# Moving half of an embedding gate from one token block's expert rows to the next block's

## The chip, the core and the metric

The kernel runs on one core of a Trainium2 chip. The metric is device time in microseconds (us) of one launch; less is better. TensorE (PE) does matmuls, VectorE (DVE) and ScalarE (ACT) elementwise work, GpSimd (POOL) issues the gathers and SyncE (SP) the weight loads. All of them run their own instruction streams and meet at semaphores.

## The reference

Two layers over 256 tokens of width 1024, all float32. Each layer has a token mixer (attention, pooling and a gated DeltaNet, merged by gates) and then a channel mixer, which is where the change lies:

```python
h = layer_norm(alpha*h + mixer(h))
q = (h @ w_q)                                    # 8 heads, two halves of 128
# top 16 + top 16 of 128 keys each, top 16 of their sums -> idx, softmax -> wts
act = gelu(einsum('thkd,td->thk', u_tab[idx], h))
ffn = einsum('thk,thkd->td', act * wts, v_tab[idx])
ple = sigmoid(h @ ple_gate) * (p @ ple_proj)     # the embedding gate
h = layer_norm(alpha*h + ffn + ple)
```

Each token reads 8 heads x 16 experts, and each expert is one row of `u` and one of `v`, 2 x 1024 numbers that lie side by side in memory.

## The kernel before, in words

The 256 tokens are two blocks of 128. Within a layer the token mixer comes first. Then come the expert rows: 128 of block 0 (head r = 0..7, rank i = 0..15, written (r, i) below), then 128 of block 1. One "row" is one gather of 128 x 2048 floats, 1 MB: for each of the 128 tokens the expert of that head and rank.

A row passes through four engines. POOL issues the gather into one of 8 slots (L670 in block 0, L688 in block 1) when the slot's earlier row has been weighed (`row_used`). DVE takes the dot product of the `u` half with `h` (L1692, L1722). ACT makes gelu(dot), times the weight, and a 128x128 diagonal matrix of it (L1289 to L1293; L1313 to L1319). PE multiplies the diagonal with the `v` half, two 512-column matmuls that add into `acc`, a PSUM tile of 128x1024 (L894, L913); each matmul shows as two in the trace, so a row is x4. Beside the dot products DVE chooses the experts of a head two ahead, in small pieces, one behind each row; ACT's exponential for it swaps the activation table twice a head, behind row 12.

Block 0's rows are written out row by row, in an order that `steps()` lists; `beside` puts other work behind chosen rows: queries and scores of later heads, the embedding projection (`pp`, L1158), and the embedding gate. The gate is 8 quarters: for each half c of the 1024 columns four quarters j of the contraction (`("pgw", c, j)`, 8 matmul records each, L789), for both blocks of tokens at once. Step `("pg", c, b)` is then ACT's sigmoid out of PSUM (L1449) and DVE's merge: `base = base*gate` (L1927) and `base = alpha*h + base` (L1928). `ACT_STEPS` and `DVE_STEPS` take it one and two rows later than it stands in the list. The quarters of c = 0 are behind rows (5,7), (5,12), (5,15), (6,4) and those of c = 1 behind (6,6), (6,9), (6,12), (7,4). Their weights come by SP, 0.5 MB a quarter (L612): seven of the eight before the rows, the last when the first quarter has been multiplied.

Between the blocks `acc` changes owner: DVE waits for block 0's last matmul, adds `acc` to `base[:, 0]` (L1675), and only then may PE start block 1, with an identity matmul that puts `base[:, 1]` into `acc` (L906).

Block 1's rows are loops: a `Fori` over heads on POOL (8 turns) and PE (7), ACT and DVE (6); the heads at the end are written out again. DVE normalises block 0 beside head 6 and makes the next layer's first columns beside head 7. Then block 1 is normalised and the next layer starts.

## Time and profile before

| | us |
|---|---|
| median of 3 runs | 1884.93 |
| lowest, highest | 1883.52, 1886.23 |
| span of the profiled execution | 1882.7 |
| PE busy | 1708.0 (91%) |
| DVE busy | 1367.7 (73%) |
| ACT busy | 905.3 (48%) |
| POOL busy | 682.3 (36%) |

The profiled execution's own time is known by its span, 1882.7 us from the first to the last instruction; the timed runs lie 0.8 to 3.5 us above that. The page counts an engine as busy while one of its instructions runs. "DMA share" is how much of the time the core's 16 DMA engines had a packet under way, and GB/s is what they moved. The page's slices are 47 us each: slices 6 to 19 are layer 1's expert rows (about 294 to 938 us), slices 26 to 39 layer 2's (about 1227 to 1872 us). In a timeline the brackets say how long the engine had been idle and what ended that; `<-DMA` means that the gather's landing did, so such a start is also the landing's time.

### The profile page before, as it was taken

Reading aid. Unit: us, or ns where it says so; the run is one execution under the profiler, and the core shown is the slowest. Engines: PE = TensorE matmul, PEld = TensorE weight load, DVE = VectorE, ACT = ScalarE, POOL = GpSimd, SP = SyncE. Lnnn points to the kernel's source line nnn. Section 1 sums busy time; section 2 is a strip of 40 time slices with the busy share of each in tenths; the row PEclk is TensorE's granted clock in tenths of the full one; section 3 lists DMA queues with packets and bytes.
Section 4 is the critical chain, followed back from the end, with each engine's and each line's share of the span. In section 5 each row is a group of like instructions: output and inputs, shape, how many; then the busy total and the mean of one; then the engine's idle time right before and its main releaser. Section 6 shows DMA issues by size and latency. Waiting matters only on the chain.

```text
span 1882.7 us, 26286 instructions
## 1 busy us (share of the span) xinstructions
PE 1708.0 (91%) x7264; PEld 980.8 (52%) x7264; DVE 1367.7 (73%) x3499; ACT 905.3 (48%) x2247; POOL 682.3 (36%) x585
## 2 busy tenths in 40 slices
PE   8999999999999878878799999999999998887876
PEld 7987887544444222223389778865443432322222
DVE  5887768877777777776468876687777787777754
ACT  5656543444444444445355665335445454444443
POOL 0110003444344455555311100044444455555553
PEclk9999999999999999999999999999999999999999
DMA  6543769999999999999955347799999999999997
GB/s 247 182 126 134 259 231 402 416 427 426 427 426 413 427 427 428 427 428 427 411 180 169 125 163 243 265 413 410 427 426 427 426 408 420 427 427 428 427 427 306
DMA packets 106728, 660.59 MB, mean 351 GB/s; under 512 B 11888, under 2 KB 12288, under 8 KB 40064
## 3 DMA queue, kind: packets, MB, share of 16 engines
q0 software_dynamic: 75376, 546.57, 69.3%
q1 hardware_dynamic: 31248, 112.74, 17.8%
q8 instruction: 52, 0.85, 0.2%
q14 instruction: 52, 0.43, 0.1%
HBM read 658.20 MB, written 1.06 MB: 350 GB/s over the span
## 4 chain that ended last, share of the span: by engine, by line
PE 46%; DMA 23%; issue 16%; DVE 8%; ACT 5%; POOL 1%; DVEq 1%; ACTq 0%; POOLq 0%; SPq 0%
PE acc L894 12%; DMA arena<-experts_dram,idxu 11%; DMA cst<-experts_dram,stage 8%; PE psum L726 5%; PE psum L727 5%; PE psum L728 5%; PE acc L913 4%; DMA arena<-experts_dram,stage 4%; PE psum L757 3%; PE psum L789 2%; DVE arena L1692 2%; PE acc L726 1%; PE acc L727 1%; PE acc L728 1%; PE psum L816 1%
## 5 line engine op out<-in xcount | busy, mean ns | idle before, releaser
L913 PE MATMUL acc<-arena 128*128 128x512 f32 x896 | 443.9, 624 | 115.3 <-ACT arena L1319 112.5
L894 PE MATMUL acc<-arena 128*128 128x512 f32 x896 | 412.0, 601 | 24.7 <-ACT arena L1293 24.5
L688 POOL DMA_INDIRECT arena<-experts_dram,stage x224 | 299.4, 1337 | 228.5 <-PE acc L913 166.7
L1722 DVE CUSTOM_DVE_ANT_0 arena<-arena,h 128x1024 f32<-128x1024 f32 x224 | 274.7, 1226 | 141.5 <-issue 61.9
L913 PEld LDWEIGHTS acc<-arena 128*128 128x128 f32 x896 | 158.9, 194 | 397.4 <-issue 397.3
L1692 DVE CUSTOM_DVE_ANT_0 arena<-arena,h 128x1024 f32<-128x1024 f32 x224 | 274.7, 1226 | 119.6 <-DMA arena<-experts_dram,idxu 115.8
L670 POOL DMA_INDIRECT arena<-experts_dram,idxu x224 | 244.9, 1093 | 304.7 <-PE acc L894 269.8
L894 PEld LDWEIGHTS acc<-arena 128*128 128x128 f32 x896 | 163.2, 189 | 252.0 <-issue 153.3
L1571 DVE TENSOR_TENSOR raw_r<-raw,w_hi_r 128x1024 fp32r<-128x1024 f32 x150 | 177.6, 1220 | 64.1 <-ACT w_hi_r L1199 63.4
L1313 ACT ACTIVATE gel<-dots 128x1 f32<-128x1 f32 x256 | 51.9, 203 | 294.6 <-DVE dots L1722 293.5
L1199 ACT ACTIVATE w_hi_r<-raw 128x1024 fp32r<-128x1024 f32 x152 | 153.9, 1053 | 49.9 <-DMA raw<-weights_dram 47.6
L1289 ACT ACTIVATE gel<-dots 128x1 f32<-128x1 f32 x256 | 51.3, 200 | 233.2 <-DVE dots L1692 232.0
L1319 ACT ACTIVATE arena<-cst,gw 128x128 f32<-128x128 f32 x256 | 102.8, 401 | 41.7 <-ACT gw L1316 17.7
L1293 ACT ACTIVATE arena<-cst,gw 128x128 f32<-128x128 f32 x256 | 102.8, 402 | 8.4
L726 PE MATMUL psum<-w_hi_r,hidden_r 128*128 128x512 f32 x256 | 102.0, 398 | 4.3 <-DVE raw_r L1571 3.4
L727 PE MATMUL psum<-raw_r,hidden_r 128*128 128x512 f32 x256 | 100.3, 392 | 0.0
L728 PE MATMUL psum<-w_hi_r,hidden_r 128*128 128x512 f32 x256 | 100.3, 392 | 0.0
L726 PE MATMUL psum<-hidden_r,w_hi_r 128*128 128x256 f32 x320 | 91.4, 286 | 0.0
L727 PE MATMUL psum<-hidden_r,w_hi_r 128*128 128x256 f32 x320 | 90.5, 283 | 0.0
L728 PE MATMUL psum<-hidden_r,raw_r 128*128 128x256 f32 x320 | 90.5, 283 | 0.0
L1316 ACT ACTIVATE gw<-gel,wst 128x1 f32<-128x1 f32 x256 | 75.4, 294 | 24.6 <-ACT gel L1313 1.7
L661 POOL DMA_DIRECT2D lnr<-lnrows_dram x2 | 1.1, 538 | 221.0 <-DVE h L1564 221.0
(296 smaller groups left out, 2710.9 us busy)
## 6 DMA issues: line engine op xcount, KB each, us to landing
raw<-weights_dram SPq DMA_DIRECT2D x168, 512.0 KB, 3.7
arena<-weights_dram SPq DMA_DIRECT2D x20, 512.0 KB, 4.6
w_hi<-weights_dram SPq DMA_DIRECT2D x12, 512.0 KB, 5.0
lnr<-lnrows_dram POOLq DMA_DIRECT2D x4, 1024.0 KB
arena<-experts_dram,idxu POOLq DMA_INDIRECT x224
arena<-experts_dram,stage POOLq DMA_INDIRECT x224
lnr<-cum_dram POOLq DMA_DIRECT2D x2, 1024.0 KB, 9.1
cst<-weights_dram SPq DMA_DIRECT2D x4, 512.0 KB, 5.5
```

The costliest lines, as they stand in the source:

```text
L670: nc.gpsimd.indirect_dma_start(slots[n % RING][:, :], None, experts[:, :], bass.IndirectOffsetOnAxis(idxu[:, n:n + 1], 0)).then_inc(slot_i ...
L688: nc.gpsimd.indirect_dma_start(slots[i % RING][:, :], None, experts[:, :], bass.IndirectOffsetOnAxis(stage[:, i:i + 1], 0)).then_inc(slot_ ...
L726: mm(dst, left[0], right[0], start=start, stop=False)
L727: mm(dst, left[0], right[1], start=False, stop=False)
L728: return mm(dst, left[1], right[0], start=False, stop=stop)
L894: last = mm(acc[:, c * 512:(c + 1) * 512], diag[:, i % 4, :], slots[n % RING][:, D + c * 512:D + (c + 1) * 512], start=n == 0, stop=n == R ...
L913: last = mm(acc[:, c * 512:(c + 1) * 512], diag[:, i % 4, :], slots[i % RING][:, D + c * 512:D + (c + 1) * 512], start=False, stop=ends)
L1199: AC(w_hi[:, n % HIS, :], raw[:, raw_slot(L, piece), :], ACT.Copy).then_inc(w_hi_ready, 1)
L1293: AC(diag[:, i % 4, :], ident, ACT.Copy, scale=gw[:, i:i + 1]).then_inc(diag_ready, 1)
L1571: TT(w_lo[:, s, :], raw[:, s, :], w_hi[:, n % HIS, :].bitcast(F32), ALU.subtract).then_inc(w_lo_ready, 1)
L1692: nc.vector.tensor_tensor_reduce(slot[:, 0:D], slot[:, 0:D], h[:, 0, :], 1.0, 0.0, ALU.mult, ALU.add, dots[:, i:i + 1]).then_inc(dot_ready, 1)
L1722: nc.vector.tensor_tensor_reduce(slots[i % RING][:, 0:D], slots[i % RING][:, 0:D], h[:, b, :], 1.0, 0.0, ALU.mult, ALU.add, dots[:, i:i + ...
```

## The change

- The four quarters of c = 0 go behind (5,7), (5,13), (6,5), (6,11), and their sigmoid and merge stand at (7,0) in the list.
- The four quarters of c = 1 leave block 0. PE makes them in block 1 behind rows (0,4), (0,10), (1,0), (1,6) (`GATE_AT`), six rows apart; ACT's sigmoids go behind row (1,11) and DVE's merge behind row (1,13).
- For that the first `OPENING = 2` heads of block 1 are written out on PE, ACT and DVE, and the loops of these engines do two turns fewer. POOL's loop stays as it is.
- Block 0's upper 512 columns have no gate yet when `acc` must be freed. DVE saves `alpha*h + acc` of these columns in `first_sums`, a free place in `hidden`, where it did `base + acc` before; the merge later adds it to `base*gate`.
- PE puts only the lower half of `base[:, 1]` into `acc` at block 1's start, and the upper half at the first row of its last head, by another wait on `base_ready`, which now counts 4 a layer.

The diff, cut to its core (`gate_quarter` is the body that stood under `kind == "pgw"`, `gate_out` and `gate_in` replace the branches for `pg`; `OPENED` keeps ACT's and DVE's main loops from doing `("pg", 1, b)` again):

```diff
     beside |= {(hd - 3, 6): [("sc", 0, hd), ("sc", 1, hd)] for hd in range(4, EH)}
     beside |= {(4, 12): [("pp", 0, 0), ("pp", 1, 0)], (5, 3): [("pp", 0, 1), ("pp", 1, 1)]}
-    beside |= {at: [("pgw", 0, j)] for j, at in enumerate(((5, 7), (5, 12), (5, 15), (6, 4)))}
-    beside |= {at: [("pgw", 1, j)] for j, at in enumerate(((6, 6), (6, 9), (6, 12), (7, 4)))}
-    beside |= {(6 + c, 5): [("pg", c, 0), ("pg", c, 1)] for c in range(2)}
+    beside |= {at: [("pgw", 0, j)] for j, at in enumerate(((5, 7), (5, 13), (6, 5), (6, 11)))}
+    beside |= {(7, 0): [("pg", 0, 0), ("pg", 0, 1)]}
     for r in range(EH):
         for i in range(TOPK):
             s += [("row", r, i)] + beside.get((r, i), [])
-    s += [("ln2", 0), ("experts", 1), ("ln2", 1)]
+    s += [("pg", 1, 0), ("pg", 1, 1), ("ln2", 0), ("experts", 1), ("ln2", 1)]
     return s
+OPENING = 2
+GATE_AT = ((0, 4), (0, 10), (1, 0), (1, 6))
+GATE_OUT, GATE_IN = 11, 13
 
 
...
         diag = at(17760, 512).rearrange("p (i n) -> p i n", i=4)
         emb_gate = at(18272, 2048).rearrange("p (b d) -> p b d", b=2)
+        first_sums = hidden[:, KT * T:KT * T + 512]
         tiu = sb("tiu", 32, U32)[:, :].rearrange("p (s k) -> p s k", s=2)
         posu = sb("posu", TOPK, U32)
...
                 read(L, g, j, ends[1])
 
+            def gate_quarter(L, c, j):
+                blocks = []
+                for b in range(2):
+                    bk, use = place(L, ("pg", c, b))
+                    if j == 0:
+                        pe.wait_ge(bank_drained[bk], use)
+                    blocks.append((psum[:, bk, :], b))
+                embedding_piece(L, GROUP_OF["pg", c, 0], j, blocks)
+                if j == 3:
+                    for b in range(2):
+                        ends[b].then_inc(bank_filled[place(L, ("pg", c, b))[0]], 1)
             def turn(L, b, q):
 
...
                         n0 = (L * NB + b) * RANKS
                         pe.wait_ge(acc_drained, L + 1)
-                        pe.wait_ge(base_ready, L * NB + 2)
-                        for c in range(2):
-                            mm(acc[:, c * 512:(c + 1) * 512], ident, base[:, 1, c * 512:(c + 1) * 512], start=True, stop=False)
-                        def weigh(r, i, ends):
-                            pe.wait_ge(diag_ready, r * TOPK + (n0 + i + 2))
+                        pe.wait_ge(base_ready, 4 * L + 2)
+                        mm(acc[:, 0:512], ident, base[:, 1, 0:512], start=True, stop=False)
+                        def weigh(r, n1, i, begins=False, ends=False):
+                            pe.wait_ge(diag_ready, r * TOPK + (n1 + i + 2))
                             pe.nop(nofuse=True)
                             for c in range(2):
-                                last = mm(acc[:, c * 512:(c + 1) * 512], diag[:, i % 4, :], slots[i % RING][:, D + c * 512:D + (c + 1) * 512], start=False, stop=ends)
+                                last = mm(acc[:, c * 512:(c + 1) * 512], diag[:, i % 4, :], slots[i % RING][:, D + c * 512:D + (c + 1) * 512], start=begins and c == 1, stop=ends)
                                 if ends and c == 0:
                                     last.then_inc(acc_half, 1)
                             last.then_inc(acc_filled if ends else row_used, 1)
 
-                        with pe.Fori(0, EH - 1) as r:
+                        for r in range(OPENING):
                             for i in range(TOPK):
-                                weigh(r, i, False)
+                                weigh(r, n0, i, begins=r + i == 0)
+                                if (r, i) in GATE_AT:
+                                    gate_quarter(L, 1, GATE_AT.index((r, i)))
+                        with pe.Fori(0, EH - 1 - OPENING) as r:
+                            for i in range(TOPK):
+                                weigh(r, n0 + OPENING * TOPK, i)
                         for i in range(TOPK):
+                            if i == 0:
+                                pe.wait_ge(base_ready, 4 * L + 4)
+                                mm(acc[:, 512:D], ident, base[:, 1, 512:D], start=False, stop=False)
                             if i == 3 and L + 1 < DEPTH:
                                 for q in range(2):
                                     turn(L + 1, 0, q)
-                            weigh(EH - 1, i, i == TOPK - 1)
+                            weigh(EH - 1, n0, i, ends=i == TOPK - 1)
                         pe.wait_ge(acc_filled, L * NB + b + 1)
                         pe.sem_inc(row_used, 1)
...
                 AC(w_hi[:, n % HIS, :], raw[:, raw_slot(L, piece), :], ACT.Copy).then_inc(w_hi_ready, 1)
 
+            def gate_out(L, c, b):
+                act.wait_ge(*filled(L, ("pg", c, b)))
+                AC(emb_gate[:, b, c * 512:(c + 1) * 512], bank(L, ("pg", c, b)), ACT.Sigmoid).then_inc(drained(L, ("pg", c, b))[0], 1)
             def columns_hi(L, b, q):
 
...
                         AC(first_gate, first_gate, ACT.Sigmoid).then_inc(late_ready, 1)
                         continue
-                    if kind in ("outa", "select", "shares", "stats", "wqh", "pgw"):
+                    if kind in ("outa", "select", "shares", "stats", "wqh", "pgw") or step in OPENED:
+                        continue
+                    if kind == "pg":
+                        gate_out(L, *step[1:])
                         continue
                     if step in (("softplus",), ("tr", 0, 0), ("onorm", 0), ("mT", 0, 0), ("ln2", 1)):
...
                                     act.nop(nofuse=True)
                                     AC(texp, texp, ACT.Exp).then_inc(texp_ready, 1)
+                                if not looped and r == 1 and i == GATE_OUT:
+                                    for blk in range(2):
+                                        gate_out(L, 1, blk)
                                 if i == 5 and beside == "columns":
                                     for q in range(2):
...
                                     inv_sqrt(rstd[:, :], mv[:, 1:2], mv[:, 1:2], rstd_ready)
 
-                        turns = EH - AHEAD
+                        turns = EH - AHEAD - OPENING
+                        for r in range(OPENING):
+                            head(r, "select", False)
                         with act.Fori(0, turns) as r:
                             head(r, "select")
...
                 TT(lo, bank(L, step).rearrange("p (k t) -> p k t", k=4), hi.bitcast(F32), ALU.subtract).then_inc(bank_drained[place(L, step)[0]], 1)
 
+            def gate_in(L, c, b):
+                cs = slice(c * 512, (c + 1) * 512)
+                dve.wait_ge(*drained(L, ("pg", c, b)))
+                dve.wait_ge(*drained(L, ("pp", c, b)))
+                link(TT(base[:, b, cs], base[:, b, cs], emb_gate[:, b, cs], ALU.mult))
+                if c and not b:
+                    dve.wait_ge(acc_drained, L + 1)
+                    made = TT(base[:, b, cs], base[:, b, cs], first_sums, ALU.add)
+                else:
+                    made = STT(base[:, b, cs], h[:, b, cs], ALPHA, base[:, b, cs], ALU.mult, ALU.add)
+                made.then_inc(base_ready, 1)
             def read_both(L, b, c):
 
...
                             continue
                         dve.wait_ge(acc_filled, L * NB + 1)
-                        dve.wait_ge(base_ready, L * NB + 1)
-                        for c in range(2):
-                            cs = slice(c * 512, (c + 1) * 512)
-                            last = TT(base[:, 0, cs], base[:, 0, cs], acc[:, cs], ALU.add)
-                        last.then_inc(acc_drained, 1)
+                        dve.wait_ge(base_ready, 4 * L + 1)
+                        TT(base[:, 0, 0:512], base[:, 0, 0:512], acc[:, 0:512], ALU.add)
+                        STT(first_sums, h[:, 0, 512:D], ALPHA, acc[:, 512:D], ALU.mult, ALU.add).then_inc(acc_drained, 1)
                         dve.wait_ge(acc_drained, L + 1)
                         continue
...
                     if kind == "experts":
                         b = step[1]
-                        n0 = (L * NB + b) * RANKS
 
                         def head(r, beside, looped):
 
+                            ahead = OPENING if looped else 0
+                            n0 = ((L * NB + b) * EH + ahead) * TOPK
                             choose = iter(())
                             if beside == "select":
-                                choose = select_head(L, r + (b * EH + AHEAD), r if looped else None)
+                                choose = select_head(L, r + (b * EH + ahead + AHEAD), r if looped else None)
                             elif beside == "norm":
+                                dve.wait_ge(base_ready, 4 * L + 3)
                                 choose = itertools.chain(statistics(base[:, 0, :]), norm(base[:, 0, :], base[:, 0, :], 0, L * 4 + 3, h2_ready))
                             for i in range(TOPK):
...
                                 nc.vector.tensor_tensor_reduce(slots[i % RING][:, 0:D], slots[i % RING][:, 0:D], h[:, b, :], 1.0, 0.0, ALU.mult, ALU.add, dots[:, i:i + 1]).then_inc(dot_ready, 1)
                                 next(choose, None)
+                                if not looped and r == 1 and i == GATE_IN:
+                                    for blk in range(2):
+                                        gate_in(L, 1, blk)
                                 if i == 5 and beside == "columns":
                                     for q in range(2):
...
                                 pass
 
-                        turns = EH - AHEAD
+                        turns = EH - AHEAD - OPENING
+                        for r in range(OPENING):
+                            head(r, "select", False)
                         n = links[0]
                         with dve.Fori(0, turns) as r:
...
                         head(EH - 2, "norm", False)
                         head(EH - 1, "columns" if L + 1 < DEPTH else None, False)
+                        continue
+                    if kind == "pg":
+                        if step not in OPENED:
+                            gate_in(L, *step[1:])
                         continue
                     if kind in NO_BANK:
```

## Rows read from the trace of the kernel before

**Rows 1.** The page's 40 slices of the span, 47 us each: DMA busy tenths and GB/s.

```profile
DMA  6543769999999999999955347799999999999997
GB/s 247 182 126 134 259 231 402 416 427 426 427 426 413 427 427 428 427 428 427 411 180 169 125 163 243 265 413 410 427 426 427 426 408 420 427 427 428 427 427 306
```

**Rows 2.** Busy time by stretch (columns in the first line).

```profile
core 0: us, PE busy (x) PEld busy (x) DVE busy (x) ACT busy (x) POOL busy (x), PEclk, DMA share, GB/s
570.00:600.00 30.00, 30.00 (x71) 13.26 (x70) 21.79 (x58) 13.86 (x41) 16.62 (x14) 1.00 1.00 404
1500.00:1530.00 30.00, 30.00 (x71) 13.30 (x70) 22.77 (x72) 14.37 (x42) 16.17 (x12) 1.00 0.99 396
1580.00:1860.00 280.00, 222.22 (x455) 80.45 (x455) 195.95 (x535) 122.96 (x370) 162.61 (x128) 0.98 1.01 427
```

**Rows 3.** The chain of waits: start, duration, what.

```profile
536.92 3.43 PE psum L789 x8
...
697.53 1.28 ACT L1313
...
736.77 1.28 ACT L1313
```

**Rows 4.** VectorE's timeline: first and last row of blocks (start, duration, instruction, wait).

```profile
302.90 1.22 DVE L1692 CUSTOM_DVE_ANT_0 arena<-arena,h 128x1024 f32<-128x1024 f32 x1 [2.53 <-DMA arena<-experts_dram,idxu]
...
620.47 1.23 DVE L1692 CUSTOM_DVE_ANT_0 cst<-cst,h 128x1024 f32<-128x1024 f32 x1 [0.71 <-DMA cst<-experts_dram,idxu]
...
937.95 1.23 DVE L1722 CUSTOM_DVE_ANT_0 cst<-cst,h 128x1024 f32<-128x1024 f32 x1 [1.98 <-issue]
...
1235.90 1.22 DVE L1692 CUSTOM_DVE_ANT_0 arena<-arena,h 128x1024 f32<-128x1024 f32 x1 [2.70 <-DMA arena<-experts_dram,idxu]
...
1553.98 1.23 DVE L1692 CUSTOM_DVE_ANT_0 cst<-cst,h 128x1024 f32<-128x1024 f32 x1 [0.71 <-DMA cst<-experts_dram,idxu]
...
1871.98 1.22 DVE L1722 CUSTOM_DVE_ANT_0 cst<-cst,h 128x1024 f32<-128x1024 f32 x1 [1.19 <-issue]
```

**Rows 5.** VectorE's timeline in the stretches of rows 2 with fewer bytes.

```profile
590.82 1.23 DVE L1692 CUSTOM_DVE_ANT_0 arena<-arena,h 128x1024 f32<-128x1024 f32 x1 [0.86 <-DMA arena<-experts_dram,idxu]
...
600.88 1.22 DVE L1692 CUSTOM_DVE_ANT_0 cst<-cst,h 128x1024 f32<-128x1024 f32 x1 [0.73 <-DMA cst<-experts_dram,idxu]
...
1517.26 1.23 DVE L1692 CUSTOM_DVE_ANT_0 arena<-arena,h 128x1024 f32<-128x1024 f32 x1 [2.17 <-DMA arena<-experts_dram,idxu]
...
1534.41 1.23 DVE L1692 CUSTOM_DVE_ANT_0 cst<-cst,h 128x1024 f32<-128x1024 f32 x1 [0.66 <-DMA cst<-experts_dram,idxu]
```

**Rows 6.** DMA queues, packets and MB: two rows of 310 to 628, one of 664 to 900.

```profile
q8 instruction: 7, 0.11, 0.1%
q14 instruction: 13, 0.11, 0.1%
...
q14 instruction: 1, 0.01, 0.0%
```

**Rows 7.** Timelines of POOL (issues) and VectorE (the row issued).

```profile
496.72 0.94 POOL L670 DMA_INDIRECT arena<-experts_dram,idxu  x1 [1.54 <-PE acc L894]
511.76 1.23 DVE L1692 CUSTOM_DVE_ANT_0 arena<-arena,h 128x1024 f32<-128x1024 f32 x1 [0.87 <-DMA arena<-experts_dram,idxu]
...
1520.62 1.13 POOL L670 DMA_INDIRECT arena<-experts_dram,idxu  x1 [3.49 <-PE acc L894]
1529.57 1.22 DVE L1692 CUSTOM_DVE_ANT_0 arena<-arena,h 128x1024 f32<-128x1024 f32 x1 [0.74 <-DMA arena<-experts_dram,idxu]
...
1566.23 0.98 POOL L685 COPY stage<-idxu 128x8 uint32 x1 [5.28 <-PE acc L913]
```

**Rows 8.** Timelines of VectorE and ScalarE: the block switch, gate read and merge.

```profile
601.95 1.09 ACT L1449 ACTIVATE arena<-psum 128x512 f32<-128x512 f32 x2
602.95 0.69 DVE L1927 TENSOR_TENSOR arena<-arena 128x512 f32<-128x512 f32 x1
...
625.70 1.28 DVE L1675 TENSOR_TENSOR arena<-arena,acc 128x512 f32<-128x512 f32 x2 [4.00 <-issue]
```

More of the change, by code:

```diff
@@ L203 @@
 DVE_STEPS = rows_later(("pg",), 2)
+OPENED = [("pg", 1, b) for b in range(2)]
 FILLS = [s for s in STEPS if s[0] not in NO_BANK]
@@ L934, in _ @@
                     if kind == "pgw":
-                        _, c, j = step
-                        blocks = []
-                        for b in range(2):
-                            bk, use = place(L, ("pg", c, b))
-                            if j == 0:
-                                pe.wait_ge(bank_drained[bk], use)
-                            blocks.append((psum[:, bk, :], b))
-                        embedding_piece(L, GROUP_OF["pg", c, 0], j, blocks)
-                        if j == 3:
-                            for b in range(2):
-                                ends[b].then_inc(bank_filled[place(L, ("pg", c, b))[0]], 1)
+                        gate_quarter(L, *step[1:])
                         continue
@@ L1446, in _ @@
                         last = AC(scs[:, b, 2 * hd:2 * hd + 2, :], ps[:, 0:2 * P].rearrange("p (l n) -> p l n", l=2), ACT.Copy)
-                    elif kind == "pg":
-                        _, c, b = step
-                        last = AC(emb_gate[:, b, c * 512:(c + 1) * 512], ps, ACT.Sigmoid)
                     elif kind == "pp":
@@ L1921, in _ @@
                             nc.vector.bn_stats(bst1[:, b, 0:6], rr[:, b, 0:512])
-                    elif kind == "pg":
-                        _, c, b = step
-                        cs = slice(c * 512, (c + 1) * 512)
-                        dve.wait_ge(*drained(L, step))
-                        dve.wait_ge(*drained(L, ("pp", c, b)))
-                        link(TT(base[:, b, cs], base[:, b, cs], emb_gate[:, b, cs], ALU.mult))
-                        last = STT(base[:, b, cs], h[:, b, cs], ALPHA, base[:, b, cs], ALU.mult, ALU.add)
-                        if c:
-                            last.then_inc(base_ready, 1)
 def constants():
```

8 lines of the change are left out of this document (4 added, 4 removed).

## The prediction

> **What bounds the kernel now.** I read the page's slices first. In both layers the expert rows run with DMA at 9 tenths and 427 GB/s, while the mixer before them moves 125 to 265 GB/s [rows 1]. Next I read the busy times by stretch: in 280 us of layer 2's block 1 PE is busy 222, DVE 196, ACT 123, and DMA share is 1.01 [rows 2]. So the expert rows wait for bytes. The chain of waits confirms it: in block 1 the head marks (an ACT table load behind the same row of each head) stand 736.77 - 697.53 = 39.24 us apart [rows 3]. That is 39.24 / 16 = 2.4525 us a row, 1.05 MB at 427.6 GB/s. I call this the clean pace. A change here can gain only where the rows fall behind it, and it costs nothing while they keep it.
>
> DVE's timeline gives how far they fall behind [rows 4]. Block 0 of layer 1, first row to last: 620.47 - 302.90 = 317.57 us for 127 rows, against 127 x 2.4525 = 311.47: 6.10 us lost. Layer 2: 1553.98 - 1235.90 = 318.08: 6.61 lost. Block 1, from block 0's last row: 937.95 - 620.47 = 317.48 for 128 rows (313.92 clean): 3.56 lost, and 1871.98 - 1553.98 = 318.00: 4.08 lost. All four blocks together leave 20.35 us.
>
> The place that the change addresses is seen twice. The chain runs on PE from 536.92, through gate quarters of 3.43 us [rows 3], and in the last thirty us of the gate PE is busy 30.00 of 30 while GB/s falls to 404 and 396 [rows 2]. In bytes that is (427 - 404)/427 x 30 = 1.62 us and (427 - 396)/427 x 30 = 2.18 us, 3.80 together. That is what the change seems to have to win.
>
> But the rows themselves hardly notice [rows 5]. In layer 1 five rows start from 590.82 to 600.88, 10.06 / 4 = 2.515 us each: 0.25 us behind the clean pace in all. In layer 2 eight rows from 1517.26 to 1534.41 take 17.15 / 7 = 2.450 us: nothing. A row counts when the last of the 16 engines has brought its part. My reading is that some engines run dry there and one has still a queue, so that the bytes missing are those of engines that were ahead. The row starts show the pace, the averages don't show which engine sets it.
>
> **The change, part by part.**
>
> *Gate quarters leave block 0.* Four quarters of 3.43 us [rows 3] go, 13.7 us of PE a layer, and the four that stay lie five or six rows apart (six at 2.4525 is 14.7 us, for 6 x 1.72 + 3.43 = 13.7 of PE, 1.72 being half a quarter's eight matmuls). PE no longer falls behind. Worth at the row starts: 0.25 us in layer 1, 0 in layer 2; by the bytes 3.80. I take 0.25, since the row starts are what the engines wait for, and keep 3.80 as the other end. The one late weight load (0.5 MB, 1.2 us at 427 GB/s) stays behind the same first quarter (5,7): 0.
>
> *Gate quarters enter block 1.* The same 3.43 us behind four rows, six apart. In block 1 PE has (280 - 222)/280 = 21% free [rows 2], 0.51 us a row, 3.0 in six rows at the paces there; at the pace of written-out rows 14.7 - 6 x 1.72 = 4.4. So each quarter about fits before the next. What queues behind it on PE are the next rows' matmuls, behind them `row_used`, then POOL's gather into that slot. The cover is the lead of the gather: at the steady state a gather issued at 496.72 is used at 511.76, 15.0 us; at the worst place of before, 1520.62 to 1529.57, 8.95, the pace was still kept [rows 7]. So about 6 us may be taken from the lead at no cost. The block switch takes 5.28 of POOL's time in layer 2 [rows 7], leaving 9.8, and four rows later the first quarter takes 3.43. Against that the written-out rows catch up: DVE needs 1.23 + 0.08 and about 0.5 of choosing, some 1.9 us a row, 0.5 less than the pace, 2 us in the four rows. 9.8 + 2.0 - 3.4 = 8.4, half a us under a lead that did no harm. I take 0; the other end is the whole quarter twice, 3.43 a layer, 6.9 in all.
>
> *Sigmoid and merge.* As many as before, at other rows. ACT: two sigmoids 1.09 us, a table load of 1.28 each way [rows 3, 8], 3.65 us behind row (1,11); behind row (1,12) the exponential with two more loads, 2.8 us. ACT has (280 - 123)/280 = 56% free, 1.4 us a row. It may be some 4 us late at row (1,13). DVE: four operations of 0.69 [rows 8], 2.8 us behind row (1,13), with some 0.5 us free a row; row (1,14) starts 2.3 late. The two overlap, since ACT waits for dots. The lead of 15.0 minus 4 stays above 8.95: 0, from -0.3 to 1 a layer. In block 0 one pair of merges now stands in head 7 alone, where before each of heads 6 and 7 had one: 0.
>
> *The switch between the blocks.* DVE waits 4.00 us for the last matmul, then two adds of 512 columns take 1.28 [rows 8]. Now one of the two is the scaled add for `first_sums`, of the same class (the merge's scaled add starts and ends like L1927's 0.69): 0. PE's identity matmul is half as long and waits for the lower halves of `base`, long done; the other half comes in head 7: 0. The new wait in head 6 (`base_ready`) is over four heads earlier: 0.
>
> *Written-out code.* This is the part that costs. PE, ACT and DVE get 2 heads x 16 rows more straight-line instructions a layer, and these are fetched through the same DMA engines that bring the rows. From 310 to 628 the trace has 7 + 13 instruction packets for nearly eight written-out heads; from 664 to 900, all loops, it has 1 [rows 6], and exactly there the pace is clean. So I ascribe the losses of rows 4 mainly to fetches that land on the engine that is last anyway. Priced by block 0: (6.10 - 1.2)/8 = 0.61 and (6.61 - 1.2)/8 = 0.68 us a head, 1.2 being the late weight load. Priced by block 1, where the loss is over one loop body and two written-out heads: 3.56/3 = 1.19 and 4.08/3 = 1.36. From below, packets that fall on engines that are ahead cost 0. Block 0's written-out heads are nearest to what is added; I take 0.65. Four heads: +2.6 us, from 0 to 5.4.
>
> The Trainium skill ("Runtime: NRT & Kernel Launch", section "Instruction fetch mechanics") speaks the other way: crossing a block of code is mostly hidden, while a taken branch breaks the sequential prefetch, so unrolling is preferred. The trace's loops, with a branch each head, hold 39.24 us a head to the last digit, so the branches cost nothing that a row sees; and the rule's "hidden" is about the engine that executes, not about the transfers beside it. By that section of the Trainium skill the code term would be 0.
>
> Sum: -0.25 + 0 + 0 + 2.6 = +2.35 on the execution's span of 1882.7, so 1885.05; the median lies 2.2 us above that span, 1884.93 + 2.35 = 1887.3.
>
> **The rivals.**
> - *The code is free*: the fetches fall on DMA engines that are ahead, and no row waits for them. For it: in the stretch around 1517 to 1534 rows keep the pace although code is written out. Against it: losses in every block with written-out heads and none in the loops. Then -0.25 remains: 1884.7. Chance 0.20. (The Trainium skill's section on instruction fetch, above, expects this one.)
> - *The bytes come back.* The engines that ran dry are the ones that count later, and the rows end earlier by up to 3.80 us. For it: rows 2. Against it: rows 5. The same mechanism acts behind the switch, where written-out rows refill the lead sooner than the loop's did: up to half of block 1's losses, 1.9 us a layer. With 0 to 2.6 for the code this gives 1877.3 (3.80 and 3.8, no code) to 1883.7, middle 1880.5. Chance 0.20.
> - *The opening of block 1 starves.* The lead after the switch falls under what the rows need when quarter (0,4) comes, and every us under it delays all later rows. It decides when the lead falls below the 8.95 us that were harmless; my estimate is 8.4, so it is near. Price 1 to 3.4 us a layer, on top of the code: 1887.3 + 2 to 6.9, middle 1891. Chance 0.15. This one is slower beyond doubt.
> - *My forecast*, code felt, nothing else: 1887.3, own range 1885.5 to 1890.3. Chance 0.45.
>
> **Numbers.** What a measurement of this kernel can tell from no change is about 0.2%, 3.8 us: faster is below 1881.2, slower above 1888.7. Faster: two thirds of the second rival, 0.13, the rest of it within. Slower: the third rival almost whole (0.13) and a quarter of my forecast's range (0.12), 0.25. Same: 0.62. Range: 1881.0 to 1891.2, which leaves out about one tenth below (the second rival's better half) and under one tenth above (half of the third).
>
> **What would show it.** In the changed kernel: (1) rows start at the clean pace and DMA is at 427 GB/s from about 570 to 600 and 1500 to 1530; block 0 loses some 0.25 and 0 us less than 6.10 and 6.61. (2) Instruction packets in the first two heads of block 1, about five a layer where the loops had three, and steps of about 1 us in the row starts there; block 1 loses 4.9 and 5.4 us in place of 3.56 and 4.08. (3) Gathers issued behind the quarters of block 1 keep 8.5 us or more to their use. I am wrong if block 0 gets shorter by over 1.5 us a layer (then the bytes counted), if block 1 loses no more than before (then the code is free), or if rows after (0,4) start over 2.6 us apart without a fetch near (then the opening starves).

## The result, and the profile after

The changed kernel takes 1888.32 us (median of 18 runs, 1886.01 to 1890.20), the kernel before 1885.59 beside it (18 runs, 1883.52 to 1888.61): a ratio of 1.0016 [1.0009, 1.0022]. That is 2.73 us slower, clear of noise but within the 0.2% called "same" ahead. The forecast was +2.35 on 1884.93, 1887.3. Of the 1.0 us between that and the result, 0.66 is the kernel before, whose median has moved with more runs; 0.38 is the sum's own.

The page of the changed kernel: DMA and GB/s in 40 slices, and the instruction queues (packets, MB, share of 16 engines).

```profile
DMA  6533769999999999999955447799999999999997
GB/s 246 184 126 135 260 231 409 421 427 426 427 427 426 415 425 409 427 427 427 407 180 173 124 162 242 265 416 416 426 427 427 426 427 416 418 419 428 427 427 299
...
q8 instruction: 55, 0.90, 0.2%
q14 instruction: 58, 0.48, 0.1%
```

The slices answer to [rows 1]. They rose where PE had been crowded (slice 13: 413 to 426, slice 33: 408 to 427) and fell where block 1's first heads now run (slices 14 and 16: 427 and 428 to 415 and 409; slices 34 to 36: 420, 427, 427 to 416, 418, 419). Both moves are of a few per cent, and only the second is felt, as the experiments show. The queues have 9 packets more (before: 52 and 52).

Busy times by stretch, the answer to [rows 2]: us, then PE, PEld, DVE, ACT, POOL busy, PE's clock, DMA share, GB/s.

```profile
570.00:600.00 30.00, 25.70 (x54) 10.29 (x53) 22.45 (x57) 17.22 (x43) 13.55 (x12) 0.94 1.01 427
1500.00:1530.00 30.00, 26.44 (x57) 10.64 (x56) 23.36 (x67) 17.18 (x43) 14.96 (x13) 0.95 1.01 426
```

The place that the change addresses is mended: PE no longer fills the stretch, and 404 and 396 GB/s have become 427 and 426. By bytes that was 3.80 us.

VectorE's timeline at the ends of the blocks, the answer to [rows 4]: start, us, instruction, and what it waited for.

```profile
301.75 1.23 DVE L1728 CUSTOM_DVE_ANT_0 arena<-arena,h 128x1024 f32<-128x1024 f32 x1 [1.52 <-DMA arena<-experts_dram,idxu]
...
619.40 1.23 DVE L1728 CUSTOM_DVE_ANT_0 cst<-cst,h 128x1024 f32<-128x1024 f32 x1 [1.18 <-DMA cst<-experts_dram,idxu]
...
939.24 1.22 DVE L1760 CUSTOM_DVE_ANT_0 cst<-cst,h 128x1024 f32<-128x1024 f32 x1 [1.99 <-issue]
...
1236.83 1.23 DVE L1728 CUSTOM_DVE_ANT_0 arena<-arena,h 128x1024 f32<-128x1024 f32 x1 [2.19 <-DMA arena<-experts_dram,idxu]
...
1554.56 1.23 DVE L1728 CUSTOM_DVE_ANT_0 cst<-cst,h 128x1024 f32<-128x1024 f32 x1 [1.20 <-DMA cst<-experts_dram,idxu]
...
1873.44 1.23 DVE L1760 CUSTOM_DVE_ANT_0 cst<-cst,h 128x1024 f32<-128x1024 f32 x1 [1.19 <-issue]
```

Subtract the clean pace (311.47 for 127 rows, 313.92 for 128) as before. The blocks now lose:

| | before | after |
|---|---|---|
| layer 1, block 0 | 6.10 | 619.40 - 301.75 = 317.65: 6.18 |
| layer 1, block 1 | 3.56 | 939.24 - 619.40 = 319.84: 5.92 |
| layer 2, block 0 | 6.61 | 1554.56 - 1236.83 = 317.73: 6.26 |
| layer 2, block 1 | 4.08 | 1873.44 - 1554.56 = 318.88: 4.96 |
| sum | 20.35 | 23.32 |

Block 1 takes 3.24 us. Block 0's -0.27 can't be told from 0: in the seven kernels below whose block 0 is that of the kernel before (1, 5 to 9, 12) single executions lose 5.01 to 9.43 us in layer 1's block 0 and 5.51 to 8.53 in layer 2's. Block 1's losses repeat far better, as a table below shows, and its +3.24 is close to the +2.73 of the medians. (The spans, 1884.2 and 1882.7, differ by 1.5 only, since in this execution layer 1's rows begin 1.15 us earlier and the way from layer 1 to layer 2 is 0.36 shorter.)

Where in block 1? The instruction packets from 622 to 745, the two heads now written out and a little more; first of the changed kernel, then of the kernel before, whose loops run there.

```profile
q14 instruction: 7, 0.06, 0.1%
q8 instruction: 1, 0.02, 0.0%
```

```profile
q14 instruction: 2, 0.02, 0.0%
```

Four of those eight stand just before steps in the landings of the rows: those at 623.2, 668.4, 710.6 and 734.3. The first has its like in the kernel before (a packet at 621.5), the other three are new. The changed kernel's VectorE timeline around the packets at 668.4 and 734.3, and around one at 690.9 that has no step:

```profile
667.13 1.22 DVE L1760 CUSTOM_DVE_ANT_0 arena<-arena,h 128x1024 f32<-128x1024 f32 x1 [0.20 <-DVE arena L1521]
670.56 1.23 DVE L1760 CUSTOM_DVE_ANT_0 arena<-arena,h 128x1024 f32<-128x1024 f32 x1 [1.86 <-DMA arena<-experts_dram,stage]
...
690.13 1.23 DVE L1760 CUSTOM_DVE_ANT_0 arena<-arena,h 128x1024 f32<-128x1024 f32 x1 [0.61 <-DMA arena<-experts_dram,stage]
692.61 1.23 DVE L1760 CUSTOM_DVE_ANT_0 arena<-arena,h 128x1024 f32<-128x1024 f32 x1 [0.53 <-DMA arena<-experts_dram,stage]
...
733.06 1.23 DVE L1760 CUSTOM_DVE_ANT_0 arena<-arena,h 128x1024 f32<-128x1024 f32 x1 [0.31 <-DMA arena<-experts_dram,stage]
736.42 1.22 DVE L1760 CUSTOM_DVE_ANT_0 arena<-arena,h 128x1024 f32<-128x1024 f32 x1 [1.64 <-DMA arena<-experts_dram,stage]
```

3.43 us apart, 2.48, and 3.36: the row behind some packets is 1 us late, behind others it isn't. The rows after it don't catch up. By the landings of the rows, the whole 5.92 us that layer 1's block 1 loses are six such steps of 0.8 to 1.1 us: at 625.1, 670.3, 713.2, 736.3, 928.5 and 939.1. The kernel before has four there, at 623.8, 654.2, 910.1 and 937.8: the one of its loop's first turn has gone and three have come. Not all are code: no instruction packet came in the 15 us before the step at 937.8, and seven loads of the next layer's weights were issued from 931 to 938. In layer 2 the changed kernel has five steps, at 1575.1, 1620.0, 1655.4, 1801.0 and 1814.5, the last of them without an instruction packet near; in the kernel before that one is at 1812.1, and the first half of the output is sent at 1804.14. Which packets count is what the experiments are about.

### The profile page after: what moved, and what is told of

Same layout as the page of the kernel before. It is cut to its first block, busy times and chain, and to the rows that moved or that the text cites. A ratio compares the mean times of both kernels' runs of the same rounds, so it can differ in the third digit from the quotient of the medians.

```text
span 1884.2 us, 25728 instructions
## 1 busy us (share of the span) xinstructions
PE 1705.5 (91%) x7264; PEld 979.9 (52%) x7264; DVE 1364.6 (72%) x3495; ACT 904.9 (48%) x2247; POOL 683.3 (36%) x585
## 4 chain that ended last, share of the span: by engine, by line
PE 53%; DMA 27%; issue 8%; ACT 5%; DVE 5%; POOL 1%; DVEq 0%; POOLq 0%; ACTq 0%; SPq 0%
DMA arena<-experts_dram,idxu 12%; PE acc L913 12%; DMA arena<-experts_dram,stage 7%; PE psum L732 7%; PE psum L733 6%; PE psum L734 6%; DMA cst<-experts_dram,stage 6%; PE acc L931 5%; PE psum L763 4%; PE acc L732 1%; PE acc L733 1%; PE acc L734 1%; PE psum L835 1%; DVE arena L1728 1%; PE psum L795 1%
## 5 line engine op out<-in xcount | busy, mean ns | idle before, releaser
L1342 ACT ACTIVATE arena<-cst,gw 128x128 f32<-128x128 f32 x256 | 102.8, 402 | 38.1 <-ACT gw L1339 10.3
```

## The experiments

Theory F (fetch): written-out code costs, whatever the gate does. Rivals: Q, the gate quarters in block 1 cost by themselves; B, the bytes missing in block 0 are worth up to 3.80 us but something hides the gain. Medians are of 11 runs, in experiments 5 and 10 of 5; "before" is the kernel before, measured beside (27 or 33 runs). A ratio needn't be that of the two medians to its last digit. The intervals are some 1.7 us wide to each side, so several single results can't be told from one another by time alone; the traces have to do that.

**1. The code without the gate.** The kernel before, with the first two heads of block 1 written out on PE, ACT and DVE. The gate stays where it was.

```diff
+OPENING = 2
 ...
-                        with pe.Fori(0, EH - 1) as r:
+                        for r in range(OPENING):
+                            for i in range(TOPK):
+                                weigh(r, n0, i, False)
+                        with pe.Fori(0, EH - 1 - OPENING) as r:
 ...
-                        turns = EH - AHEAD
+                        turns = EH - AHEAD - OPENING
+                        for r in range(OPENING):
+                            head(r, "select", False)
```

> The kernel before with the first two heads of block 1 written out on PE, ACT and DVE; the gate stays in block 0 as it was. My theory (the code that is fetched costs): block 1 loses 5 to 6 us where it lost 3.6 and 4.1, the time is 2.6 us over the kernel before (2 to 3.5), about the changed kernel's. The rival that the gate's matmuls in block 1 cost it: no change, within 0.5 us of before. The rival that code is free and faster rows refill the lead: up to 1 us faster.

Measured: 1888.75 against 1886.00, 1.0017 [1.0008, 1.0026]. The packets are 55 and 58, the changed kernel's own. The code alone makes the whole slowdown: +2.75 for +2.73 by the medians.

**2. The gate without the quarters' work.** The changed kernel, with the products of block 1's gate quarters left out but for one short pair at the end (the upper half of the gate isn't computed).

```diff
+                if c:
 ...
+                    if j < 3:
+                        pe.sem_inc(piece_used, 1)
+                        return
```

> The changed kernel without the products of block 1's gate quarters (28 of 32 matmuls a layer left out; sigmoid and merge stay, on values that aren't the gate's). My theory: the quarters in block 1 are hidden, so the time stays within 0.5 us of the changed kernel, 2.7 us over before (the left out matmuls also save a little code, 64 instructions a layer and quarter row at most). The rival that block 1's opening starves: back to the time of before.

Measured: 1888.26, 1.0015 [1.0006, 1.0024]. 28 of 32 matmuls a layer are gone, and from 622 to 745 PE is busy 99.45 us in place of 105.81 (at a mean granted clock of 0.93, for 0.99 with them). The time is still above the kernel before: Q falls as the cause.

**3 and 4. The bytes of block 0.** Twice the kernel before: once with the upper half's quarters left out in the same way (3), once with all eight quarters kept in block 0 but about five rows apart (4).

```diff
+                            if j < 3:
+                                pe.sem_inc(piece_used, 1)
+                                continue
```

> The kernel before without the products of the upper half's gate quarters in block 0 (28 of 32 matmuls a layer left out; sigmoid and merge stay). It shows what the crowded quarters in block 0 cost. My theory: GB/s stays at 427 from 570 to 600 and 1500 to 1530, but the time gains 0.3 us at most, within 0.6 us of before. The rival that the bytes count: 3.8 us faster than before.

```diff
-    ... enumerate(((5, 7), (5, 12), (5, 15), (6, 4)))}
-    ... enumerate(((6, 6), (6, 9), (6, 12), (7, 4)))}
-    beside |= {(6 + c, 5): [("pg", c, 0), ("pg", c, 1)] for c in range(2)}
+    ... enumerate(((5, 7), (5, 12), (6, 1), (6, 6)))}
+    ... enumerate(((6, 11), (7, 0), (7, 5), (7, 9)))}
+    beside |= {(6, 7): [("pg", 0, 0), ("pg", 0, 1)], (7, 10): [("pg", 1, 0), ("pg", 1, 1)]}
```

> The kernel before with the eight gate quarters spread inside block 0, about five rows apart, behind (5,7) (5,12) (6,1) (6,6) (6,11) (7,0) (7,5) (7,9); nothing goes to block 1, no code is added. My theory: within 0.6 us of before (0 to 0.3 faster). The rival that the bytes count: 2 to 3.8 us faster.

Measured: 1885.54, 0.9996 [0.9987, 1.0005], and 1885.41, 0.9999 [0.9990, 1.0008]. Busy times by stretch of kernel 4 (columns as above):

```profile
570.00:600.00 30.00, 28.61 (x66) 12.29 (x66) 22.44 (x58) 14.30 (x42) 14.91 (x13) 1.00 1.01 427
1500.00:1530.00 30.00, 28.60 (x67) 12.13 (x66) 24.00 (x70) 16.94 (x43) 11.33 (x11) 1.00 1.01 426
```

The bytes are back (404 and 396 to 427 and 426) without a line of code more, and the time stays: 3.80 us would have been a ratio of 0.9980, outside both intervals. B falls at that size; 1 or 2 us the intervals would not exclude.

How the bytes can be missing without loss is in the traces, too. They hold 16 landing marks for each gather (the updates of its semaphore), one for each of 16 parts; the row can start with the last. Experiment 7's kernel below has the crowded quarters of the kernel before, with 401 GB/s from 570 to 600. There, from row (7,4) to (7,7), the last part goes from 592.22 to 599.80, 7.58 us where the pace is 7.36, but its distance to the first part shrinks from 4.03 to 2.94. Behind the first quarter of block 1 the changed kernel shows the same: from row (0,7) to (0,10) the first parts fall back by 9.24 us (633.76 to 643.00), the last ones by 7.46 (639.82 to 647.28). So what was ahead ran dry, and what comes last went on within 0.2 us of its pace over these three rows.

**5. Twice the dose.** Experiment 1 with four heads.

```diff
-OPENING = 2
+OPENING = 4
```

> The kernel before with four heads of block 1 written out on PE, ACT and DVE in place of two; the gate stays in block 0. It is the dose. My theory: the cost goes with the code, so about twice that of two heads (which measured 1.0017, 3.2 us): 5 to 6.5 us over before, 104 + 9 + about 9 more instruction packets in the trace. The rival that the cost lies at the block switch or at the entry of the loops, once a block: the same 3 us as with two heads.

Measured: 1892.07 against 1885.52, 1.0036 [1.0022, 1.0050]; packets 57 and 66. +6.55 us for eight heads, against +2.75 for four: 0.7 to 0.8 us a head.

**6. Empty code, void.** 1024 instructions that do nothing a layer on SyncE in block 1's loops, 16 waits beside them.

```diff
+                for m in range(32, 96, 8):
+                    sp.wait_ge(row_used, RING + L * NB * RANKS + RANKS + m)
+                    for _ in range(128):
+                        sp.nop(nofuse=True)
```

> The kernel before, in which SyncE, idle during block 1, executes 1024 empty instructions a layer there, in eight groups of 128 between block 1's rows 32 and 96. Nothing waits for them; only their code has to be fetched (64 KB a layer, 8 packets of 8 KB). My theory (the transfers themselves cost): block 1 loses more in the loops where it lost nothing before, by 0.3 us a packet on average as in the kernel before (about 18 us of losses over 54 packets), 16 packets, 3 to 5 us; 0 only if they always fall on a DMA engine that is ahead. The rival that written-out heads are slow on the engines that execute them: no change.

Measured: 1885.64, 1.0002 [0.9993, 1.0011]. It says nothing: the page counts 26302 instructions against 26286, the 16 waits alone, and packets 52 and 52. The empty instructions never reached the program. Experiments 10 to 12 use semaphore increments for that reason.

**7, 8 and 9. Whose code?** Experiment 1's edit on PE alone (7), on ACT and DVE (8), on DVE alone (9).

```diff
 PE (7):
-                        with pe.Fori(0, EH - 1) as r:
+                        for r in range(OPENING):
 ...
 ACT and DVE (8), DVE (9):
-                        turns = EH - AHEAD
+                        turns = EH - AHEAD - OPENING
+                        for r in range(OPENING):
+                            head(r, "select", False)
```

> The kernel before with the first two heads of block 1 written out on PE alone. My theory: a part of the 2.7 us by its share of the code, 32 rows of some ten instructions of 64 bytes, 20 KB of about 60 KB a layer: 1 us (0.5 to 1.5). The rival that it is PE's larger packets (16 KB, 0.9 us each) that cost: nearly all of it, 2 us or more.

> The kernel before with the first two heads of block 1 written out on ACT and DVE alone, PE's loop as it was. My theory: the rest of the 2.7 us, 1.7 (1 to 2.5). The rival that PE's packets cost: under 0.7.

> The kernel before with the first two heads of block 1 written out on DVE alone (426 instructions more in the program; ACT and PE loop as before). Two heads written out on ACT and DVE measured 2.7 us more. If every fetch costs alike: 1.3 us over before. If only one engine's fetches fall on the DMA engine that is last in every row: 2.5 us (it is DVE) or 0 (it is ACT).

| | us | before | ratio | packets q8, q14 |
|---|---|---|---|---|
| 7 PE | 1886.21 | 1885.52 | 1.0005 [0.9996, 1.0014] | 55, 52 |
| 8 ACT, DVE | 1888.18 | 1885.52 | 1.0013 [1.0004, 1.0022] | 52, 58 |
| 9 DVE | 1888.41 | 1886.20 | 1.0007 [0.9998, 1.0016] | 52, 55 |

PE's code comes through q8 and the others' through q14. Expected were 1 us for 7 and 1.7 for 8; the medians give 0.7 and 2.7. The times lean to ACT and DVE, but by themselves they don't part 7 from 9. The trace does more: in kernel 9 the rows are late at the same places as in the changed kernel. The stretch of the first step, VectorE's timeline, and then the packets from 664 to 670:

```profile
666.65 1.23 DVE L1726 CUSTOM_DVE_ANT_0 arena<-arena,h 128x1024 f32<-128x1024 f32 x1 [0.93 <-DMA arena<-experts_dram,stage]
670.05 1.23 DVE L1726 CUSTOM_DVE_ANT_0 arena<-arena,h 128x1024 f32<-128x1024 f32 x1 [1.16 <-DMA arena<-experts_dram,stage]
```

```profile
q14 instruction: 1, 0.01, 0.3%
```

3.40 us where the pace is 2.45, with a packet at 667.6. The other two steps have theirs at 710.2 and 736.2. PE's and ACT's written-out heads aren't there, so these three steps need DVE's alone.

What block 1 loses in each kernel parts 7 from 9 more sharply than the times do. VectorE's rows at the ends of layer 1's block 1, kernel 7 and kernel 9:

```profile
619.58 1.23 DVE L1698 CUSTOM_DVE_ANT_0 cst<-cst,h 128x1024 f32<-128x1024 f32 x1 [0.76 <-DMA cst<-experts_dram,idxu]
...
937.05 1.23 DVE L1728 CUSTOM_DVE_ANT_0 cst<-cst,h 128x1024 f32<-128x1024 f32 x1 [1.98 <-issue]
```

```profile
621.54 1.23 DVE L1695 CUSTOM_DVE_ANT_0 cst<-cst,h 128x1024 f32<-128x1024 f32 x1 [0.73 <-DMA cst<-experts_dram,idxu]
...
941.19 1.23 DVE L1726 CUSTOM_DVE_ANT_0 cst<-cst,h 128x1024 f32<-128x1024 f32 x1 [1.98 <-issue]
```

That is 317.47 and 319.65 us, less 313.92: 3.55 and 5.73 lost. In the same way for all:

| written out in block 1's first heads | layer 1 | layer 2 | over before |
|---|---|---|---|
| nothing: before, 6, 11 | 3.56, 3.53, 3.56 | 4.08, 4.29, 4.28 | 0, 0.2, 0.2 |
| PE (7) | 3.55 | 4.48 | 0.4 |
| DVE (9) | 5.73 | 5.01 | 3.1 |
| ACT, DVE (8) | 5.57 | 4.86 | 2.8 |
| PE, ACT, DVE (1) | 5.47 | 5.10 | 2.9 |
| the same with the gate, without its products (2) | 5.55 | 5.04 | 3.0 |
| the changed kernel | 5.92 | 4.96 | 3.2 |
| four heads of PE, ACT, DVE (5) | 6.69 | 7.64 | 6.7 |

DVE's written-out heads alone take all that the changed kernel's block 1 loses over before; PE's and ACT's take nothing that can be told from 0. It is a matter of three packets: DVE's heads bring 3 more in the whole program (55 for 52), and the changed kernel's block 1 has 11 steps where kernel 7's has 8.

The landing marks show why it is DVE's. At each packet one of the 16 parts slips, and stays late in the gathers that follow. How far parts lie behind the first part of their gather, us:

| packet | rows | the part that slips | the last part |
|---|---|---|---|
| DVE's, kernel 9, 667.6 | (1,1) to (1,2) | it is the last | 3.65 to 4.62 |
| DVE's, changed kernel, 668.4 | (1,2) to (1,3) | it is the last | 4.28 to 5.25 |
| ACT's, changed kernel, 690.9 | (1,13) to (1,14) | 1.27 to 1.98 | 5.18 to 5.20 |
| PE's, changed kernel, 684.3 | (1,10) to (1,11) | to 2.10, from 1.29 or less | 5.22 to 5.21 |

(That 690.9 is ACT's is seen from kernel 8, which has a packet at 691.8, and from 7 and 9, which have none there.) In kernel 9 the other 15 parts stay within 1.61 us while the last goes on to 5.51 at (2,3) and 6.43 at (2,13), one step for each of DVE's packets. A row waits for its last part, so DVE's packets are paid in full and the others' fall into a lead.

**10 and 11. The same count of instructions on DVE and on ACT.** Four spare semaphore increments at each of block 0's rows, some 1000 instructions in all.

```diff
+        spare = [sem(f"spare{i}") for i in range(4)]
 ...
+                        for k in range(4):
+                            dve.sem_inc(spare[k], 1)      # 10; 11: act.sem_inc
```

> The kernel before with four increments of semaphores that nobody waits for behind each of block 0's rows on DVE: 1024 instructions more in the program, 64 KB, 8 packets of 8 KB. The rows' work is the same. Theory (the fetch costs, per byte as with the written-out heads, 842 instructions for 2.7 us): 3.3 us over before, with steps of 1 us at row starts behind instruction packets, more in block 0, none in block 1. Rival (written-out heads cost by how their engines run them): under 0.5 us, since DVE has 0.86 us free a row there.

> The same on ACT: 1008 instructions more, behind each of block 0's rows. Theory: 3.2 us over before if ACT's fetches cost like DVE's, 0 to 0.5 if they fall on a DMA engine that is ahead. Rival: under 0.5.

Measured: on DVE 1899.52 against 1886.20, 1.0069 [1.0056, 1.0083]; on ACT 1886.16, 0.9999 [0.9990, 1.0008]. The theory had expected 3.3 us on DVE, a quarter of the 13.3 that came. Both pages have the same packets:

```profile
q8 instruction: 52, 0.85, 0.2%
q14 instruction: 60, 0.49, 0.1%
```

ACT's eight packets more cost nothing; at 1 us each they would have been a ratio of 1.004. DVE's are not cleanly priced, since the increments also slow the engine. The waits of VectorE from 300 to 620, kernel before and kernel 10 (us in total, times, longest):

```profile
DVE arena L1692 <- DMA arena<-experts_dram,idxu: 57.6, 73, 2.5
```

```profile
DVE arena L1695 <- DMA arena<-experts_dram,idxu: 42.5, 46, 3.4
DVE arena L1695 <- DVE arena L1504: 5.8, 10, 0.9
```

It waits for rows in 46 places in place of 73, and elsewhere for itself. Steps in the landings are there as well, of 0.96 to 1.01 us at 450.0, 480.4, 510.7 and 575.1, each 2 to 3 us behind a packet. Of the 13.3 us some part is the one and some the other, and the split stays open.

**12. Foreign code in the loops.** 1024 increments a layer on SyncE while block 1's loops run; SyncE issues nothing that a row needs there.

```diff
+                for m in range(32, 96, 8):
+                    sp.wait_ge(row_used, RING + L * NB * RANKS + RANKS + m)
+                    for k in range(128):
+                        sp.sem_inc(spare[k % 4], 1)
```

> The kernel before with 1024 such increments a layer on SyncE, which has nothing else to do there, in eight groups between block 1's rows 32 and 96, where all other engines loop and the rows lose nothing: 2048 instructions, 128 KB. It takes the cost of the fetch apart from every engine that works on rows. Theory: 16 packets, 3 to 6 us, in steps of 1 us in the middle of block 1; near 0 if SyncE's fetches fall on a DMA engine that is ahead. Rival: 0, and no steps.

Measured: 1888.08 against 1886.20, 1.0010 [1.0001, 1.0019]; 68 packets on q14, 16 more than before. That is 1.9 us where 3 to 6 were expected, or near 0 if the packets fell on an engine that is ahead: it is something of both. VectorE's timeline at an early one (at 734.9) and at a late one (at 834.9):

```profile
733.57 1.22 DVE L1733 CUSTOM_DVE_ANT_0 arena<-arena,h 128x1024 f32<-128x1024 f32 x1 [0.31 <-DMA arena<-experts_dram,stage]
736.03 1.23 DVE L1733 CUSTOM_DVE_ANT_0 arena<-arena,h 128x1024 f32<-128x1024 f32 x1 [0.73 <-DMA arena<-experts_dram,stage]
...
834.19 1.22 DVE L1733 CUSTOM_DVE_ANT_0 arena<-arena,h 128x1024 f32<-128x1024 f32 x1 [0.68 <-DMA arena<-experts_dram,stage]
837.35 1.22 DVE L1733 CUSTOM_DVE_ANT_0 arena<-arena,h 128x1024 f32<-128x1024 f32 x1 [1.63 <-DMA arena<-experts_dram,stage]
```

2.46 us, the pace, and 3.16. In layer 1 the five packets up to 794.0 cost next to nothing, the one at 813.4 costs 0.2 us, those at 834.9 and 853.6 about 0.7. So code that no row waits for delays rows, by transfers alone, and first it doesn't. The trace doesn't name the DMA engine that carries a packet, but the landing marks show a lead being spent. How far the part that slips lies behind the first part of its gather, and how far the last:

| after the packet at | 734.9 | 756.4 | 774.3 | 794.0 | 813.4 | 834.9 | 853.6 |
|---|---|---|---|---|---|---|---|
| row | (3,0) | (3,8) | (4,0) | (4,8) | (5,0) | (5,8) | (6,0) |
| the part that slips | 2.12 | 2.80 | 3.49 | 4.16 | 4.81 | 5.51 | 6.17 |
| the last part | 4.66 | 4.65 | 4.66 | 4.66 | 4.81 | 5.51 | 6.17 |

Each packet puts the same part back by 0.65 to 0.70 us. Up to 794.0 another part is the last and the rows keep their pace; at 813.4 this one becomes the last, and from there on every packet is paid in full.

## Why the prediction was right

- *Gate quarters leave block 0*, -0.25 (to -3.80): right to take the small end. Block 0 changed by +0.08 and -0.35 us, which is -0.27 in all, but such a difference is far under block 0's spread between executions, so the 0.25 itself isn't shown. Experiments 3 and 4 show that the other end, the bytes, is worth nothing that can be measured. Reading row starts beside the averages decided this.
- *Gate quarters enter block 1*, 0: right (experiment 2). The lead of 8.4 us expected at the first quarter was too short. In the changed kernel the gather behind the first quarter is issued at 643.39 and its row starts at 654.94, 11.55 us; the shortest in block 1's opening (layer 2, row (0,8)) is 1566.60 to 1577.67, 11.07, so the 8.95 never came into play. The sum had charged the switch and the quarter to one gather in full. The changed kernel's chain of waits runs through the quarters all the same:

```profile
637.46 3.43 PE psum L795 x8
640.90 6.88 PE acc L931 x16
...
649.61 11.39 DMA arena<-experts_dram,stage
...
666.66 3.43 PE psum L795 x8
```

  Being on this chain isn't being what the rows wait for: it goes back through whatever released the gather at 649.61, but experiment 2 takes nearly all of the quarters' work away and block 1 still loses 5.55 and 5.04 us.
- *Sigmoid and merge*, 0: right in the price, wrong in a size. In layer 1 row (1,14) was to start 2.3 us late on DVE. It started at 702.21 and had landed at 697.31, 4.9 us late. DVE's lines and ACT's of the changed kernel:

```profile
692.59 1.28 ACT L1220 ACT_TABLE_LOAD   x1
693.88 1.08 ACT L1220 ACTIVATE arena<-psum 128x512 f32<-128x512 f32 x2
...
699.01 0.17 DVE L1563 TENSOR_REDUCE tsum<-arena 128x1 f32<-128x16 f32 x1 [1.87 <-ACT arena L1346]
699.56 0.68 DVE L1610 TENSOR_TENSOR arena<-arena 128x512 f32<-128x512 f32 x1
...
702.21 1.22 DVE L1760 CUSTOM_DVE_ANT_0 arena<-arena,h 128x1024 f32<-128x1024 f32 x1
```

ACT's sigmoids and table loads delay its exponential, and DVE's choosing waits 1.87 us for that, ahead of the merges. The two delays add up here, where I had let them overlap. The gathers issued behind it still land 10.6 us or more after their issue in layer 1, and 9.4 or more in layer 2 (row (2,6)). The steps in the landings there have their packets at 710.6 and 1653.5, and kernel 9, which has no merge there, has them too: no row paid.
- *The switch*, 0: experiment 1, with the switch as before, has the whole slowdown, so the new switch is worth nothing that can be measured beside it.
- *Written-out code*, +2.6 (0.65 a head): right, and the whole of the result. Experiment 1 measures 2.75 / 4 = 0.69 a head. The mechanism, fetches "that land on the engine that is last anyway", is what the landing marks show. "What would show it" named about 1 us a step and 4.9 and 5.4 us lost in block 1: the three new steps of layer 1 are 0.97, 1.11 and 1.00 over the pace by their landings, the losses 5.92 and 4.96, right in sum (10.9 for 10.3) but not by layer, where whole packets count: DVE's come to two more in layer 1 and one more in layer 2. I had said five packets a layer; it was eight from 622 to 745 of layer 1.
- *Luck in the 0.65*: it was priced by block 0's 6.10 and 6.61 us in one execution. By the same sum the 5.01 to 9.43 us of other executions give 0.48 to 1.03 a head, 1.9 to 4.1 us for four. That the sum came out within 0.4 us is in part luck; that the term is there isn't.
- *Whose packets*: the prediction priced all code alike and let chance decide which packet counts. That was too coarse. The new steps go with DVE's packets (9), ACT's are free (11, and 8 beside 9), and PE's cost nothing that can be told from 0 (7, up to 0.14%). That a packet of 8 KB, which occupies its engine for about 0.3 us (0.3% of 16 engines over the 6 us from 664 to 670), puts the engine's part back by about 1 us when it is DVE's and by 0.7 when it is ACT's or SyncE's remains unexplained. So does why the part that DVE's packets hit is the last one.
- *The rivals.* "The code is free" gave 1884.7: fallen by 1 and 5. "The bytes come back": fallen by 3 and 4. "The opening starves": fallen by 2 and by leads of 11 us and more in the two opened heads.

The Trainium skill ("Runtime: NRT & Kernel Launch", section "Instruction fetch mechanics") holds crossings of code blocks to be mostly hidden and prefers unrolling. For ACT's code experiment 11 agrees (0.9999 with eight packets more), and for PE's experiment 7 (1.0005 [0.9996, 1.0014]). For the three engines' code together it doesn't, because of DVE's: 1.0017 for four unrolled heads, 1.0036 for eight, in rows that wait for DMA. The sum by that rule, 1884.7, was 3.6 us off.

None of the twelve is faster than the kernel before; 4 mends the same stretch without the code and is level with it (0.9999 [0.9990, 1.0008]).

## What to carry to other kernels

Where a stretch runs at the pace of its transfers, count each head or turn that is written out as transfers of its own: here 0.7 to 0.8 us a head, where the loop cost nothing that was seen. Ask whose code it is, too: here one engine's packets made the whole loss. A dip in GB/s is a loss only if the consumer's start times slip too; read these first, and test with a version that mends the dip and adds no code. Extra work cost nothing here in code that was already written out (4).

## What the runs showed of the hardware

- Instruction packets aren't equal: 8 more on ACT's behalf cost 0 (0.9999), 16 on SyncE's 1.9 us (1.0010 [1.0001, 1.0019]), 3 of DVE's about 1 us each (block 1 loses 3.1 us more with DVE's heads alone, 0.4 with PE's alone).
- A packet puts back one of a gather's 16 parts, and rows pay only if that is the last to land: DVE's moved the last from 3.65 to 4.62 us behind the first, ACT's another from 1.27 to 1.98 with the last at 5.20.
- SyncE's packets all put back the same part, by some 0.7 us each. The first five of layer 1's loops spent its lead (it reached 4.16 us, the last part was at 4.66), the seventh and eighth were paid in full.
- GB/s over all DMA engines can fall by a few per cent without loss: 404 and 396 mended to 427 and 426 gave 0.9999 [0.9990, 1.0008].
- Semaphore increments on VectorE are not free filler: four a row, with four packets more a layer, cost 13.3 us over 256 rows, while the same on ScalarE cost nothing.
